# Attention scores of two neighbouring heads, issued together and alternating between the two partition halves

## What is computed

```python
s = jnp.einsum('bhqd,bhkd->bhqk', q, k) * 64 ** -0.5    # 256 x 256 a head, over 64 numbers
p = softmax(s + bias_of_head + mask)
y = jnp.einsum('bhqk,bhkd->bhqd', p, v)                 # 256 x 64 a head
x = layer_norm(ALPHA * x + (y * silu(gate)) @ w_out)
```

## Time and profile before

| | |
|---|---|
| median of three runs | 2304.53 us |
| the profiled execution's own time | 2303.6 us |
| its span, first to last instruction | 2301.8 us |
| granted TensorE clock, mean | 0.999 |
| instructions | 24772 |
| TensorE matmuls, busy | 2277.5 us (99%), 10640 |
| TensorE weight loads, busy | 1891.9 us (82%) |
| VectorE, busy | 1211.8 us (53%) |
| ScalarE, busy | 963.7 us (42%) |
| GpSimd, busy | 226.9 us (10%) |
| mean DMA rate | 189 GB/s |

### The profile page before, as it was taken

How to read it: one execution, slowest core, us unless ns; L and a number is a source line. 1 busy time by engine, 2 the same in 40 slices (tenths; PEclk the granted TensorE clock), 3 DMA queues, 4 the chain that set the end, 5 groups by cost and what they waited for, 6 DMA issues and landing times.

```text
span 2301.8 us, 24772 instructions
## 1 busy us (share of the span) xinstructions
PE 2277.5 (99%) x10640; PEld 1891.9 (82%) x10640; DVE 1211.8 (53%) x967; ACT 963.7 (42%) x829; POOL 226.9 (10%) x205
## 2 busy tenths in 40 slices
PE   8999999999999999999999999999999999999997
PEld 6888878888888888888888888888888888888886
DVE  4457535555555545555544444444455555555556
ACT  5454454433334434344433433433444444444432
POOL 1003100000000000000000000000000142353101
PEclk9999999999999999999999999999999999999999
DMA  7545446676767666655565565555556645555563
GB/s 253 186 143 165 146 148 202 199 212 199 212 192 205 202 203 205 225 186 183 183 199 185 184 200 183 189 195 186 188 192 207 237 161 169 182 161 165 194 235 110
DMA packets 213245, 435.60 MB, mean 189 GB/s; under 512 B 8564, under 2 KB 8784, under 8 KB 212240
## 3 DMA queue, kind: packets, MB, share of 16 engines
q1 hardware_dynamic: 205280, 408.97, 54.7%
q0 software_dynamic: 7712, 24.98, 4.4%
q10 hardware_dynamic: 144, 0.07, 0.0%
HBM read 421.93 MB, written 12.06 MB: 189 GB/s over the span
## 4 chain that ended last, share of the span: by engine, by line
PE 98%; DVE 1%; ACT 0%; DMA 0%; issue 0%; ACTq 0%; DVEq 0%; POOLq 0%
PE acc L1180 30%; PE acc L1182 30%; PE acc L1181 30%; PE side L1190 2%; PE side L1213 1%; PE side L1265 1%; PE side L1252 1%; PE side L1241 1%; PE side L1242 0%; PE side L1243 0%; DVE X L1010 0%; DMA VG<-in_g_mix 0%; DVE X L1006 0%; DVE wlo L845 0%; PE side L1324 0%; PE side L1225 0%
## 5 line engine op out<-in xcount | busy, mean ns | idle before, releaser
L845 DVE TENSOR_TENSOR wlo<-raw,whi 128x2048 fp32r<-128x2048 f32 x383 | 890.3, 2325 | 846.7 <-ACT whi L602 846.7
L602 ACT ACTIVATE whi<-raw 128x2048 fp32r<-128x2048 f32 x383 | 733.2, 1915 | 764.1 <-PE acc L1182 764.0
L1180 PE MATMUL acc<-whi,setA_lo 128*128 128x512 f32 x1792 | 703.9, 393 | 2.6 <-DVE wlo L841 2.6
L1182 PE MATMUL acc<-whi,setA_hi 128*128 128x512 f32 x1792 | 698.2, 390 | 0.0
L1181 PE MATMUL acc<-wlo,setA_hi 128*128 128x512 f32 x1792 | 698.1, 390 | 0.0
L1180 PE MATMUL acc<-whi,setB_lo 128*128 128x512 f32 x1280 | 504.1, 394 | 0.0
L1181 PE MATMUL acc<-wlo,setB_hi 128*128 128x512 f32 x1280 | 498.5, 389 | 0.0
L1182 PE MATMUL acc<-whi,setB_hi 128*128 128x512 f32 x1280 | 498.4, 389 | 0.0
L1180 PEld LDWEIGHTS acc<-whi,setA_lo 128*128 128x128 f32 x1792 | 337.1, 188 | 73.5 <-issue 4.3
L1182 PEld LDWEIGHTS acc<-whi,setA_hi 128*128 128x128 f32 x1792 | 336.9, 188 | 70.2
L1181 PEld LDWEIGHTS acc<-wlo,setA_hi 128*128 128x128 f32 x1792 | 337.2, 188 | 69.2 <-issue 1.0
(11 more groups left out here) (173 smaller groups left out, 930.9 us busy)
## 6 DMA issues: line engine op xcount, KB each, us to landing
raw<-in_w_in SPq DMA_DIRECT2D x191, 1024.0 KB, 5.2
raw<-in_w_ffn_up SPq DMA_DIRECT2D x64, 1024.0 KB, 5.2
raw<-in_w_ffn_down SPq DMA_DIRECT2D x64, 1024.0 KB, 5.1
raw<-in_w_gla_out SPq DMA_DIRECT2D x16, 1024.0 KB, 5.1
raw<-in_w_conv_out SPq DMA_DIRECT2D x16, 1024.0 KB, 5.1
raw<-in_w_o SPq DMA_DIRECT2D x16, 1024.0 KB, 5.1
raw<-in_w_out SPq DMA_DIRECT2D x16, 1024.0 KB, 5.1
t_scratch<-t5v POOLq DMA_DIRECT2D x8, 512.0 KB, 7.3
```

Of the source, the lines that this page charges most:

```text
L602: e.activation(whi[r][:, :, :], raw[r][:, :, :], ACT.Copy).then_inc(s_hi, 1)
L845: e.tensor_tensor(wlo[r][:, :, :], raw[r][:, :, :], asf(whi[r][:, :, :]), ALU.subtract).then_inc(s_lo, 1)
L1180: e.matmul(o, xl, whi[r][:, k, :], start=kk == 0, stop=False)
L1182: f = e.matmul(o, xh, whi[r][:, k, :], start=False, stop=kk == 15)
```

## The change

The scores of heads a and a + 1 are both issued in the step of an even a; odd steps issue none. TensorE takes a bank for each head and alternates matmul by matmul: one of head a on partitions 0 to 63, one of head a + 1 on 64 to 127. The number of matmuls, their sizes and operands stay. The list of bank uses, VectorE's reading of scores, ScalarE's exponentials and GpSimd's fetches of bias follow in pairs; values and probs stay where they were.

```diff
@@ side_uses
         return ([("values", a - 2)] if a >= 2 else []) + ([("probs", a - 1)] if 1 <= a <= 32 else []) \
-            + ([("scores", a)] if a < 32 else [])
+            + ([("scores", a), ("scores", a + 1)] if a < 32 and a % 2 == 0 else [])
@@ pool
-                    elif job == "att" and a + 2 < 32:
+                    elif job == "att" and a + 2 < 32 and a % 2 == 0:
                         fetch_bias(a + 2)
+                        fetch_bias(a + 3)
@@ scalar, and the same two lines in vector
-                        h = a
-                        if h < 32:
+                        for h in ((a, a + 1) if a < 32 and a % 2 == 0 else ()):
@@ tensor, scores
-                bank, done = take(("scores", h))
+                bank0, done0 = take(("scores", h))
+                bank1, done1 = take(("scores", h + 1))
                 for t in range(2):
-                    o = bank[:, 256 * t:256 * t + 256]
-                    qh, ql = (x[g % 2][q:q + 64, j, 128 * t:128 * t + 128] for x in (qTa, qTl))
-                    kh, kl = (x[g % 2][q:q + 64, j, :] for x in (kTa, kTl))
-                    e.matmul(o, ql, kh, start=True, stop=False)
-                    e.matmul(o, qh, kl, start=False, stop=False)
-                    f = e.matmul(o, qh, kh, start=False, stop=True)
-                f.then_inc(done, 1)
+                    cols = slice(256 * t, 256 * t + 256)
+                    toks = slice(128 * t, 128 * t + 128)
+                    for n, (x, y) in enumerate(((qTl, kTa), (qTa, kTl), (qTa, kTa))):
+                        f0 = e.matmul(bank0[:, cols], x[g % 2][0:64, j, toks], y[g % 2][0:64, j, :],
+                                      start=n == 0, stop=n == 2)
+                        if t == 1 and n == 2:
+                            f0.then_inc(done0, 1)
+                        f1 = e.matmul(bank1[:, cols], x[g % 2][64:128, j, toks], y[g % 2][64:128, j, :],
+                                      start=n == 0, stop=n == 2)
+                f1.then_inc(done1, 1)
@@ tensor, the order of the jobs
-                        if a < 32:
+                        if a < 32 and a % 2 == 0:
                             scores(a)
```

More of the change, by code:

```diff
@@ L1230, in scores @@
             def scores(h):
-                g, j, q = h // 8, (h % 8) // 2, 64 * (h % 2)
+                g, j = h // 8, (h % 8) // 2
                 if h % 8 == 0:
```

## The result

The changed kernel takes 2284.01 us (median of four runs, 2282.49 to 2286.07) against 2304.49 before in the same comparison: ratio 0.9911, 95% interval 0.9899 to 0.9923. That is 20.5 us less; 18.8 were forecast. The profiled execution took 2283.81 with a span of 2282.0.

The account below looks back on a forecast made before the run. TensorE, busy 99% of the span with 98% of the last-ending chain, was taken as the bound. -6.2 - 11.5 - 1.1 = -18.8 us from the median 2304.5 gave 2285.7 us, range 2283 to 2298.5.

Parts of the forecast that it names:

- Part 1: TensorE's scores: the same 192 matmuls in 16 jobs instead of 32, saving 0.39 us of row changes each, 6.2 us.
- Part 3: Effects beside TensorE's path: the wait for VectorE at a = 28 shrinks from 2.05 to some 0.9 us, counted -1.1.
- Part 2: Alternating two heads' scores matmuls on TensorE's partition halves: gain 11.5 taken; 1.9, 0 or a 35 us cost also considered.
- The upper bound: In pair jobs both halves run at once, a pair taking 0.12 us like one matmul: 96 x 0.12 = 11.5 us gained.
- the reason that tipped it: After the drain before scores, the second weight load waits for the first load's end; a half of its own has none.
- Rival (b): Changing half drains TensorE between neighbours in a pair job: 35 us cost, about 2332 us in all; chance 0.07.
- the term of VectorE's product with the gate: VectorE's chain before a = 28: gate ends at 2122.08, the product with it at 2124.5, the read at 2127.3.
- The covers: Slack for later softmax, weight splits and bias fetches: about 6 us on VectorE, 1.4 on GpSimd; nothing reaches TensorE.
- the cover of 1.4: GpSimd: a pair's two bias fetches take 13.8 us and fit before the next need by 1.4 us.
- (a): Pair jobs: weight loads of two halves go one by one, gaining 1.9 or nothing; 2295.3 or 2298.3 us; chance 0.32.
- (c): New TensorE waits at transposes or products eat the gain, 7 us; 2305 without overlap, 2293.8 with; chance 0.08.
- (d): Partial overlap in pair jobs, a pair of matmuls in about 0.18 us: 2291.5 us; chance 0.07.

## Why the prediction was right

**What bounds.** Right: TensorE at 99% and 98% of the chain, before and after.

**Part 1, -6.2.** Right. Sixteen "issue" places instead of 32; the odd steps have none. Grouping without overlap (both heads on one half) shortened the stage from 331.8 to 322.7 us, by 9.1: 6.2, the two waits of together 2.65 (Part 3), none of which is left there, and a rest of 0.3. Its median, 2294.63, is 10.1 under the 2304.7 of before in that comparison; the 1.0 between 9.1 and 10.1 is not explained.

**Part 2, -11.5 against 1.9 or 0 or +35.** The upper bound was right to 0.01 us a job (1.46 for 1.47), 11.4 us by the run on one half. The choice of it was in part luck. The prediction said itself that the rows don't decide, and the reason that tipped it was weak and misread: the second load there starts at 1859.05, before the first one's recorded end (1858.94 + 0.18 = 1859.12), so the row shows no waiting for that end. What decides is shown now: loads of the two halves start together, as do the matmuls. The Trainium skill, "TensorE: Matmul & The Clock Gate" (The mechanism), had the overlap right; its statement in the same section that matmuls start strictly in program order differs from the run with blocks of five, where head a + 1's first matmul starts at 1852.84, ahead of the third, fourth and fifth of head a (the third at 1852.95), which stand before it in the program. The measurement decides. Rival (b) is out: a change of the number of rows and back costs 0.35 to 0.39, a change of half nothing.

**Part 3, -1.1.** The mechanism was right, the size was off: the waits together cost 2.05 at a = 28 and 0.6 at a = 4, and went to 0.2, so about -2.4 (2.65 less 0.2). The 0.6 is read from the timeline of TensorE in the kernel before: the second four transposes could follow the first after 0.44, at 1868.18.

```profile
1867.74 0.66 PE L1190 MATMUL side<-ident,tmp 128*128 128x128 f32 x4
1868.78 0.66 PE L1190 MATMUL side<-ident,tmp 128*128 128x128 f32 x4 [0.38 <-DVE Y L1127]
```

The step that was mis-sized is the term of VectorE's product with the gate, which I took with the 2.38 us of the earlier trace rows. After the change it lasted 1.29 (timeline of VectorE):

```profile
2107.62 1.29 DVE L971 TENSOR_TENSOR tmp<-Y,tmp 128x512 f32<-128x512 f32 x2 [0.79 <-ACT tmp L667]
```

Of the eight halves of this product in the kernel before seven took 0.69 us and one 1.77, the second of the two in the earlier trace rows. GpSimd's add of the mask ran at the same time (2125.21 to 2126.90), but it ran beside most of the first half too, which took 0.69; that it stretched the second is argued, not shown. And I left the wait at a = 4 as it was, though I had written that VectorE is earlier there too.

**The covers.** No wait of TensorE for a split of weights, an exponential or a bias came up; the 0.2 above is all. Two fetches of bias took 12.1 us in the third group of heads (2001.90 to 2014.00) where I had 13.8. In the fourth group the first pair took 15.7 (2083.93 to 2099.58), more than the cover of 1.4 allows, and VectorE's second reading of scores began right behind the add (timelines of GpSimd and VectorE):

```profile
2098.29 1.29 POOL L503 TENSOR_TENSOR bia<-bia,msk 128x512 f32<-128x512 f32 x1 [3.69 <-DMA bia<-rb_scratch]
```

```profile
2099.67 0.69 DVE L1139 SCALAR_TENSOR_TENSOR Sm<-side,bia 128x512 f32<-128x512 f32 x1
```

That reading started 2.26 us after the first one (2097.41), where 1.56 is usual. VectorE's cover took it, as the prediction said of this case, and TensorE lost nothing.

**Sum.** The forecast was 1.7 us short, 1.3 of it from Part 3. Jobs: (2 x 1.11 - 1.10) x 16 = 17.9, waits 2.4, together 20.3, and the stage gave 20.4. The median moved by 20.5. That the median agrees with the stage to 0.1 us is luck: the changed kernel's runs lie 3.6 us apart, and the two profiles' spans differ by 19.8 (2301.8 to 2282.0), since a fall of the clock ahead of the stage comes in between. Rivals (a), (c) and (d) did not come.

## What to carry to other kernels

Where matmuls use 64 rows or fewer, put independent ones on different row halves (or quarters) and into different banks (one bank for both was not tried), near each other in the queue: they run at once, float32 weight loads included. Strict alternation isn't needed, up to four of one half may stand in a row. Gather them, since every change between 128 and 64 rows costs TensorE about 0.2 us, the uncovered load included. Where TensorE waits for an engine that is late, look two engines back: here a softmax of ScalarE, ahead of a gate in its queue, cost 2 us at one place. Moving it gave back 1.4 us, since a smaller wait came up elsewhere.

## What the runs showed of the hardware

- Two halves of 64 rows load and multiply at once: 12 matmuls of 64 rows by 256 columns in six places of 0.12 us, their weight loads started together; 12 places where both use one half (1.46 against 2.17 us a job).
- TensorE starts matmuls of the other half ahead of their turn. Behind one that has been handed over three more of its half can stand, a fourth holds up what follows. Blocks of 3 and 4: 0.01 to 0.02 us between the halves; of 5: 0.23 us; of 6: 0.35 us.
- So matmuls of different halves don't always start in program order (blocks of five), and "works through its queue in order", as said of the engines at the start, does not hold for TensorE between halves.
- A change from 128 to 64 rows and back costs 0.35 to 0.39 us.
- Four quarters run at once as well, also for float32 matmuls of 16 rows: 16 records in 0.8 instead of 3.3 us.
- Behind a stretch of 3.5 us with matmuls of 16 rows the granted clock fell to its lower level in five of ten profiles, for 1.6 us of time in four of them (3.1 in the fifth). With the matmuls issued twice it fell in the one profile, and the four runs had the lowest mean clocks (0.995 to 0.997). With them spread over four quarters it did not fall in the one profile.
